# Index units ahead of the convolution units, index dots among the convolution units, and masked sums in pairs

## The reference, cut to what matters

```python
z = jnp.einsum('btd,dn->btn', h, w_in_l)
q, k, v, ga, qi, wi, ki, ub, gb, cv, cg, gc = split_columns(z)
q = partial_rope(rms_norm(q.reshape(...), q_norm_g_l), pos)      # 8 heads of 64; k the same
uc = cv * jax.nn.sigmoid(cg)                                     # GLU of the convolution branch
...
dots = jnp.einsum('bqhd,bsd->bqhs', qi, ki) * (D_IDX ** -0.5)    # indexer: 8 heads of 32
sc = jnp.einsum('bqh,bqhs->bqs', w, jax.nn.relu(dots))
sc = jnp.where(adm[None], sc, -jnp.inf)
_, idx = lax.top_k(sc, top_k)                                    # 132 keys of a prompt query
...
s = jnp.einsum('bqhd,bqkhd->bqhk', q, k_sel) * (HEAD_DIM ** -0.5)
s = jnp.where(valid[:, :, None, :], s, -jnp.inf)
p = jax.nn.softmax(s, axis=-1)
return jnp.einsum('bqhk,bqkhd->bqhd', p, v_sel)
```

## Time and profile before

| what | value |
|---|---|
| median of 3 runs | 752.42 us (747.38 to 752.99) |
| the profiled execution, its own time | 746.28 us |
| its span in the profile | 745.0 us |
| PE busy | 702.3 us, 94% |
| DVE busy | 523.2 us, 70% |
| ACT busy | 331.2 us, 44% |
| POOL busy | 300.3 us, 40% |
| mean granted clock of PE | 0.984 |
| read from HBM | 64.05 MB, 96 GB/s over the span with writes |

### The profile page before, as it was taken

One profiled execution on the slowest core, in us unless ns is written; L12 is line 12 of the kernel. 1 busy time (PEld: TensorE's weight loads), 2 busy tenths in 40 slices (PEclk: granted clock), 3 DMA queues, 4 the chain that ended last, 5 costly groups with the idle time before them and its releaser, 6 DMA issues.

```text
span 745.0 us, 13366 instructions
## 1 busy us (share of the span) xinstructions
PE 702.3 (94%) x4690; PEld 567.3 (76%) x4690; DVE 523.2 (70%) x1320; ACT 331.2 (44%) x850; POOL 300.3 (40%) x445
## 2 busy tenths in 40 slices
PE   5899999999889999998999999999988799999998
PEld 5897756578777777776999866666878688777797
DVE  3538888899977977435663898989997777822232
ACT  5525646533947333334132555543485643332212
POOL 1013698942848710011120459895376763000000
PEclk9999999999989999999999999999999899999999
DMA  5543040314232536014025304031522244501203
GB/s 195 160 137 118 17 128 30 114 35 143 58 87 60 179 136 227 1 58 139 21 92 153 126 4 142 30 88 46 157 58 61 83 151 167 170 1 57 96 22 112
DMA packets 54979, 71.90 MB, mean 97 GB/s; under 512 B 12977, under 2 KB 30585, under 8 KB 54881
## 3 DMA queue, kind: packets, MB, share of 16 engines
q1 hardware_dynamic: 54802, 70.96, 30.0%
q10 hardware_dynamic: 111, 0.08, 0.0%
HBM read 64.05 MB, written 7.61 MB: 96 GB/s over the span
## 4 chain that ended last, share of the span: by engine, by line
PE 70%; DVE 21%; ACT 3%; issue 2%; DMA 2%; POOL 1%; SPq 0%; ACTq 0%; DVEq 0%; POOLq 0%
PE R L1273 16%; PE R L1260 6%; PE R L1244 6%; PE R L1262 6%; PE R L1261 6%; PE R L1245 6%; PE R L1246 6%; DVE bias L1715 5%; DVE small L1713 5%; PE R L1409 4%; PE A L1360 3%; PE A L1213 2%; PE A L1438 2%; DVE W_r L1614 2%; PE R L1213 1%
## 5 line engine op out<-in xcount | busy, mean ns | idle before, releaser
L1260 PE MATMUL R<-x_hi,W_r 128*128 128x268 f32 x448 | 137.7, 307 | 5.9 <-DVE bufA L1614 3.3
L1262 PE MATMUL R<-x_hi,W_r 128*128 128x268 f32 x448 | 133.3, 297 | 0.0
L1261 PE MATMUL R<-x_lo,W_r 128*128 128x268 f32 x448 | 133.0, 297 | 0.0
L1244 PE MATMUL R<-W_r,x_hi 128*128 128x512 f32 (+3 forms) x320 | 123.0, 385 | 3.3 <-DVE W_r L1614 3.3
L1273 PE MATMUL R<-yT,W 128*128 128x268 f32 (+2 forms) x768 | 124.2, 318 | 1.0 <-DVE gt L1882 1.0
L1273 PEld LDWEIGHTS R<-yT,W 128*128 128x128 f32 x768 | 106.9, 190 | 16.8 <-issue 6.2
L1245 PE MATMUL R<-W_r,x_hi 128*128 128x512 f32 (+3 forms) x320 | 118.4, 370 | 0.0
L1246 PE MATMUL R<-W_r,x_lo 128*128 128x512 f32 (+3 forms) x320 | 118.1, 369 | 0.0
L823 POOL TENSOR_TENSOR W_r<-W,W_r 128x256 fp32r<-128x256 f32 x112 | 79.4, 742 | 53.1 <-ACT W_r L940 52.3
L1260 PEld LDWEIGHTS R<-x_hi,W_r 128*128 128x128 f32 x448 | 89.5, 200 | 14.5 <-issue 8.5
L1261 PEld LDWEIGHTS R<-x_lo,W_r 128*128 128x128 f32 x448 | 89.9, 201 | 0.0
(11 more groups left out here) (259 smaller groups left out, 1219.7 us busy)
## 6 DMA issues: line engine op xcount, KB each, us to landing
W<-in_w_in SPq DMA_DIRECT2D x52, 512.0 KB, 4.7
KV<-in_cache_k SPq DMA_DIRECT2D x32, 256.0 KB, 3.0
W<-in_w_out SPq DMA_DIRECT2D x8, 1024.0 KB, 6.6
KV<-in_cache_v SPq DMA_DIRECT2D x32, 256.0 KB, 3.9
ubx<-qkv_rows SPq DMA_DIRECT2D x16, 256.0 KB, 3.5
W<-in_w_in SPq DMA_DIRECT2D x8, 296.0 KB, 3.5
out_new_k_prompt<-kz SPq DMA_DIRECT2D x8, 256.0 KB, 2.2
out_new_v_prompt<-V SPq DMA_DIRECT2D x8, 256.0 KB
```

The source lines that it names most:

```text
L1244: pe.matmul(out, x_hi[:, kc, rows], hi, start=(kc == 0), stop=False)
L1260: pe.matmul(out, hi[:, cols], x_hi[:, kc, toks], start=(kc == 0), stop=False)
L1261: pe.matmul(out, hi[:, cols], x_lo[:, kc, toks], start=False, stop=False)
L1262: m = pe.matmul(out, lo[:, cols], x_hi[:, kc, toks], start=False, stop=(kc == KC - 1))
```

## The change

**What it does.** The idx group comes first: its four loads of two blocks are the first loads of all (AHEAD is 4 of such, where it was 2 of four blocks), and the idx units run in the tile order 1, 2, 0, 3, 4. Then the row of token scales and the state transposes; then the conv units, with the index transposes behind the first three of them and a pair of dots after every second kc of the last five (DOTS_OF). Dots go round four PSUM banks (A[p % 4]), so that PE may be two pairs ahead of DVE. DVE's gathers and ACT's relus stand beside those conv units, and all 31 taps in the k and q stretch, with selections beside the k units too. The splits of the weights are moved accordingly. SP issues the loads 10 to 13 behind the stores of the index keys, not ahead of them. At the turn of the layers two of the four first loads go to the ring as before, the others, once attention is through with V, to V's space, and are split by ACT behind the loop and by DVE between the last output units. In attention DVE does the masked sums of items n and n + 1 back to back at even n below 32, where it did one at each n. POOL's list is the same but for the order of the index tiles.

```diff
-GROUPS = [("cv", C_CV, 256, 4), ("cg", C_CV + 256, 256, 4), ("idx", C_I, 296, 2), ("k", C_K, 512, 2), ("q", C_Q, 512, 2),
+GROUPS = [("idx", C_I, 296, 2), ("cv", C_CV, 256, 4), ("cg", C_CV + 256, 256, 4), ("k", C_K, 512, 2), ("q", C_Q, 512, 2),
...
+IDX_ORDER = (1, 2, 0, 3, 4)
+IDX_NTH = {i: n + 1 for n, i in enumerate(IDX_ORDER)}
+EARLY = ([("idx", i, 0) for i in IDX_ORDER]
+         + CONV_ORDER
...
-IX_K, IX_Q = 4, 4
+DOTS_OF = {("conv", 1, 1): 0, ("conv", 2, 0): 8, ("conv", 2, 1): 16, ("conv", 3, 0): 24, ("conv", 3, 1): 32}
+assert len(PIECES) == 40
...
-REST_J = (3, 7)
-TAPS_IDX, TAPS_K, TAPS_Q = 8, (3, 3, 3, 3, 3), (2, 2, 2, 1, 1)
+TAPS_K, TAPS_Q = (3, 3, 3, 3, 3), (3, 3, 3, 3, 4)
...
+            for m in range(8, 10):
                 w_load(m)
-            for i in range(NT):
-
-                sp.wait_ge(*idxz_s.at(i + 1))
+            for i in IDX_ORDER:
...
+            for m in range(10, 14):
+                w_load(m)
...
-                for m in range(AHEAD):
+                for m in range(2):
...
+                for m in range(2, AHEAD):
+                    next_w.did(sp.dma_start(w_raw(m, W, 1), w_source(l + 1, m)))
...
+            high(4)
+            high(5)
...
+            for i in IDX_ORDER:
+                idx_evac(i)
+            row_keep()
+            act.wait_ge(*st_t.at(1))
+            st_k.did(copy(uxs[:, :, :, 0:CONV_STATE], A[:, 0, 0:480].rearrange("p (c b j) -> p c b j", c=2, b=8)))
+            act.wait_ge(*st_t.at(2))
+            st_k.did(copy(ubs[:, :, :, 0:POOL_STATE], A[:, 1, 0:240].rearrange("p (c b j) -> p c b j", c=2, b=8)))
             high(6)
             high(7)
...
+            for n in range(5):
+                for p in range(8 * n, 8 * n + 8):
+                    relu(p)
+                if n:
+                    high(7 + n)
+                if n == 3:
+                    half_tanh(0)
+            half_tanh(1)
...
+                    if u in DOTS_OF and kc % 2 == 1:
+                        dots(DOTS_OF[u] + kc - 1)
...
+            def dots(first):
+
+                if first == 0:
+                    pe.wait_ge(*idxk_s.at(NT))
+                    pe.wait_ge(*row_s.at(3))
+                elif first >= 4:
+                    pe.wait_ge(*acc_s.at(first - 2))
+                for p in (first, first + 1):
+                    i, h, lo, hi = PIECES[p]
+                    b = 32 * (h % 4)
+                    ix_s.did(pe.matmul(A[0:ROWS[i], p % 4, 0:hi - lo], qkT[b:b + 32, h // 4, START[i]:START[i] + ROWS[i]],
+                                       qkT[b:b + 32, 2, lo:hi], start=True, stop=True))
...
+            turns_behind = {("conv", 0, 0): (1, 2), ("conv", 1, 0): (0, 3), ("conv", 0, 1): (4,)}
+            for u in CONV_ORDER:
+                unit_fm(u, ("cv", "cg")[u[1] // 2], 128 * (u[1] % 2))
+                if u == ("conv", 0, 0):
+                    pe.wait_ge(*st_k.at(2))
+                for i in turns_behind.get(u, ()):
+                    idx_turn(i)
...
-                unit_tm(("k", i, 0), "k", 4 * i)
+                unit_tm(("k", i, 0), "k")
                 if i >= 2:
                     kq_turn(i - 2)
             for i in range(NT):
-                unit_tm(("q", i, 0), "q", 4 * NT + 4 * i)
+                unit_tm(("q", i, 0), "q")
...
+                if u in DOTS_OF:
+                    for p in range(DOTS_OF[u], DOTS_OF[u] + 8):
+                        gather(p)
...
+                if u in (("conv", 0, 0), ("conv", 1, 0)):
+                    rest(6 + m)
+                if m >= 2:
+                    rest(8 + 2 * (m - 2) + h)
...
+            j = 0
             for i in range(NT):
-                for x in range(0, IX_K, 2):
-                    gather(p)
-                    gather(p + 1)
-                    p += 2
-                    for _ in range(TAPS_K[i] // 2 if x else (TAPS_K[i] + 1) // 2):
-                        tap(j)
-                        j += 1
+                for x in range(TAPS_K[i]):
+                    tap(j)
+                    j += 1
+                between(2)
...
+                for x in range(TAPS_Q[i]):
+                    tap(j)
+                    j += 1
+                kq_sum(NT + i)
+                between(2)
...
+                if n < PAIRED and n % 2 == 0:
+                    masked(n)
+                    masked(n + 1)
+                elif PAIRED <= n < len(ITEMS):
+                    masked(n)
...
+                if l + 1 < DEPTH and m < 4:
+                    dve.wait_ge(*next_hi.at(m + 5))
+                    split_rest(dve, l + 1, 2 + m // 2, m % 2, next_lo)
```

294 lines of the change are left out of this document (115 added, 179 removed).

## The result

The changed kernel takes 777.89 us (median of 4 runs, 772.73 to 781.47) where the kernel before takes 751.46 (4 runs): a ratio of 1.0355, with a 95% interval of 1.0281 to 1.0430. It is 26.4 us slower. The profiled execution of the changed kernel took 779.1 us with a span of 777.8, 32.8 above the span of before; that pair overstates the medians' difference, as the profiled execution of before was among the fastest of its kernel. The forecast was 762, with a range up to 777: the direction was right, the size was not.

A forecast was written before the change was run, and what follows sets the result against it. PE was taken to set the pace, with POOL's serial chain under a microsecond ahead of its need. Terms of +7.2 us a layer and start and turn gains summed to +11.9 on 746.28, 758.2; forecast 762, range 745 to 777.

The forecast's parts named there:

- POOL's chain (part 1): k to v stretch: POOL's 76.4 us serial chain doesn't shrink, PE waits some 14 us; +12.2 us a layer with dots moved.
- rival B: k to v stretch: POOL's tiles shorten without DVE's gathers beside them, its chain does not bind; 734 to 743 us; chance 0.10.
- The dots' price (part 1): Dots moved from k/q units into conv units: 20 pairs cost PE 15.0 us a layer, as many as before, only earlier.
- Conv units (part 2): Conv units: DVE nearly full, PE waits after evacuations and splits in three of five units; +1.9 us a layer, bounds 0 to 10.
- rival C: Conv units bound by DVE through dots, relu, gather: 10 instead of 1.9 us a layer, 778 us; chance 0.11.
- The start (part 3): Kernel start: PE waits 4.1 us at the fifth index unit, index transposes' waits go; -0.5 us layer 0, -0.8 layer 1.
- DVE's lead (part 4): Start of attention: DVE is ready before PE, so early waits on the masked sum go; -3.8 us a layer.
- The pairs and what follows item 10 (part 4, 5): Later attention: paired masked sums shorten waits before scores, -2.2 us a layer; clock terms -1.7 and +0.8.
- -2.2 a layer: Later attention: waits before scores shrink by the scores PE may run before needing DVE, 0.8 + 0.5 + 0.9 us.
- A rule weighed and used too narrowly: DVE instructions with two SBUF inputs block POOL; denser taps cost POOL nothing, or 13 us a layer if they blocked too.
- The clock (part 5): Attention: slow clock after waits goes with DVE's lag, -1.7 us a layer; new waits in v units +0.8.
- The offset: Whole kernel: forecast 762 set 3.8 us above the 758.2 sum, nearer 764.3, the sum added to the median run.

The follow-up runs named there:

- no_gain: Changed kernel without POOL's multiplication of the k and q tiles by the norm's gain; 747.46 us, ratio 0.9927.
- before_no_gain: Kernel before without POOL's multiplication of the k and q tiles by the norm's gain; 752.75 us, ratio 1.0017.
- before_two_gains: Kernel before with POOL's multiplication of the k and q tiles by the norm's gain done twice; 769.35 us, ratio 1.0251.
- rest_late: Changed kernel with POOL's weight subtractions for loads 26, 27 behind the first block of cache products, 28, 29 behind the second; 768.95 us, ratio 1.0230.
- long_run: Changed kernel with POOL's weight subtractions for loads 26 and 27 ahead of its powers, behind those for 24 and 25; 769.08 us, ratio 1.0237.
- pair_only: Kernel before with only the masked sums of items n and n + 1 back to back at even n below 32; 747.80 us, ratio 0.9956.
- diff_10: Changed kernel with the first half of DVE's pooling differences at step 10 of the attention loop, not 9; 777.63 us, ratio 1.0349.
- rest_late_eps: rest_late with the addition of EPS to the sums of squares done by DVE, not POOL; 768.67 us, ratio 1.0169.
- before_long_run: Kernel before with POOL's weight subtractions for loads 26 and 27 ahead of its powers, behind those for 24 and 25; 752.08 us, ratio 1.0009.

## Why the prediction was wrong

- **POOL's chain (part 1).** Right. Its end, and not PE, now closes the stretch from the first k matmul to the last q transpose. The stretch was to take 86.7 us and took 86.96 and 86.94; PE's waits on kz and W_r are 21.9 us. no_gain, before_no_gain and before_two_gains show that the chain's length sets its pace, and rival B (it does not bind) fell.
- **The dots' price (part 1).** Mis-sized: 15.0 a layer taken over from the k units. In a conv unit the pair costs more, as one of 400 columns shows on PE of the changed kernel:

```profile
439.28 0.28 PE L1272 MATMUL R<-x_hi,W_r 128*128 128x268 f32 x1
439.49 0.94 PE L1317 MATMUL A<-qkT 32*128 32x400 f32 x4
440.36 0.39 PE L1270 MATMUL R<-x_hi,W_r 128*128 128x268 f32 x1
440.59 0.28 PE L1271 MATMUL R<-x_lo,W_r 128*128 128x268 f32 x1
```

  From 439.28 to 440.36 are 1.08 us, less 0.12 for the matmul itself, and the next start comes 0.23 and not 0.12 behind: 1.07 for a pair whose busy time is 0.94, where between 512-wide matmuls gap and busy time agreed. In all about 17 a layer (an estimate, 15.0 x 1.07 / 0.94; the turn of the layer has 104.16 - 86.09 = 18.1 us more of PE busy, some of it clock), 4 us for both.
- **Conv units (part 2).** Smaller than forecast: 0.9 us of waits a layer on DVE's bias, where 1.9 was taken, and nothing of rival C. That the measured 777.9 meets the 778 of that rival is chance: its mechanism is not in the trace.
- **The start (part 3).** Right: the wait of 4.1 us at the fifth idx unit came as 4.14, at 33.71 where 34.1 was worked out.
- **DVE's lead (part 4).** Right as far as it was seen: at the scores of item 10 the changed kernel had won 14.8 - 10.8 = 4.0 us against before, the forecast was 3.8; and the masked sums come right behind the scores.
- **The pairs and what follows item 10 (part 4, 5).** This is the step that failed. "-2.2 a layer" took each wait before scores as caused by the masked sum. The waits before scores did go, 17.1 us down to 0.8. But behind item 10 the changed kernel lost 5 to 6 us a layer by the held instruction, for which the sum has no term, and the wait at 261.93 was handed back since DVE was waiting there for POOL's cache products. Both were to be seen in the trace of before: the list of DVE's waits has 4.9 us on KV in it, and one yT<-gt,yT lasted 1.90 us where its others take 0.44, to 214.16, just behind the end of POOL's run at 213.87. Attention was forecast 6.9 us a layer shorter and came out 3.8 and 0.9 longer; moving POOL's run alone gave 9 us back over both layers (rest_late, long_run).
- **A rule weighed and used too narrowly.** The Trainium skill (SBUF — State Buffer, "Who interferes with whom") also says that the order of issue decides which of the two engines blocks. I asked only what DVE's instructions would do to POOL's tiles. The traces agree that DVE can be the one that is blocked. They don't bear out that the order of issue alone decides: DVE's instruction is recorded from 219.34 on, the run's first from 219.81, and yet DVE's was held through all eight.
- **The clock (part 5).** The 1.7 us a layer that a higher clock was to give did not come: the granted clock over attention of layer 0 is 0.96 against 0.98 before, and PE is busy 150.98 us in it against 148.57. Other waits stand where the first ones were; that they keep the clock down is likely, not shown. In the k to v stretch its 3.5 us were hidden behind POOL, as forecast.
- **The offset.** I put the forecast 3.8 us above the sum, because the median lay above the profiled execution. It is in part luck that this was the right way: the medians' difference of 26.4 is smaller than the profiles' 32.8 because the profiled execution of before was one with a high clock, 0.984. With 8.9 us for the hold added, the forecast of 762 would be 770.9, still short of 777.9.

## What to carry to other kernels

Where two engines are level in a stretch, work taken out of it from one of them wins nothing there and is paid in full where it is put: ask for the serial chain of each engine, from its first instruction to its last, before moving anything. A wait is won only if what is late next is late for another reason: look at what the engine named in the wait was itself waiting for. And when an order is shifted by a few microseconds, list what POOL runs back to back, and which DVE instructions with two inputs from SBUF will now stand beside it. Compare runs at the same granted clock before a small gain is put down to an edit: pair_only, which leaves POOL's and PE's order alone, is the fastest version that leaves nothing out by the medians (0.9956, 0.9924 to 0.9988), but between profiles at one clock its gain is not seen.

## What was unexpected in the hardware

A DVE instruction whose two inputs are in SBUF can be held until the end of a run of POOL instructions that follow each other without a gap: 6.01 to 6.04 us for 64x30 elements that else take 0.2, 5.02 in diff_10, 10.05 for 128x268 in rest_late_eps, each ending 0.03 to 0.3 us behind the run. Instructions with one input in PSUM, as the masked sums, pass beside the same runs at their usual time (0.29 us for 128x144 at 211.23 in the kernel before, inside the run that ends at 213.87). It does not always happen: in before_long_run such instructions passed a run of 12.4 us with 0.5 us of delay each at most. The kernel before missed it by 0.6 us of arrival, and two kernels had it in one layer and not in the other. What a hold costs the whole differs too: 2 to 4.5 us a layer in the changed kernel, while the attention of before_two_gains, with a hold in each layer, is in sum 1 us longer than before.
